# Up projection of a gated MLP with matmuls of 512 and 256 columns, and other short matmuls ahead of its units

## What is computed

```python
def conv_glu_ffn(h, w_up, w_conv, w_down):
    up = causal_dwconv(h @ w_up, w_conv)      # h (256, 2048), w_up (2048, 11264)
    g, u = jnp.split(up, 2, axis=-1)
    return (jax.nn.silu(g) * u) @ w_down      # w_down (5632, 2048)

x = x + conv_glu_ffn(rmsnorm(x, norm_ffn[l]), ffn_up[l], ffn_conv[l], ffn_down[l])
```

## Time and profile before

| | us |
|---|---|
| median of 3 runs | 1977.06 |
| lowest and highest run | 1976.96, 1981.57 |
| the profiled execution's own time | 1976.82 |
| its span in the trace | 1974.9 |
| PE busy | 1960.4 (99%) |
| DVE busy | 1179.8 (60%) |
| ACT busy | 868.4 (44%) |

### The profile page before, as it was taken

One profiled execution on the slowest core, in us unless ns is written; L12 is line 12 of the kernel. 1 busy time (PEld: TensorE's weight loads), 2 busy tenths in 40 slices (PEclk: granted clock), 3 DMA queues, 4 the chain that ended last, 5 costly groups with the idle time before them and its releaser, 6 DMA issues.

```text
span 1974.9 us, 38712 instructions
## 1 busy us (share of the span) xinstructions
PE 1960.4 (99%) x16939; PEld 1951.9 (99%) x16939; DVE 1179.8 (60%) x1292; ACT 868.4 (44%) x789; POOL 40.3 (2%) x62
## 2 busy tenths in 40 slices
PE   8999999999999999999999999999999999999999
PEld 8999999999999999999999999999999999999999
DVE  5677644545454376576655345777777777754443
ACT  5446334434374343455444444534344433333333
POOL 1000100000000000000000000000000000000000
PEclk9999999999999999999999999999999999999999
DMA  8666754665657757565564456665656565566664
GB/s 271 209 203 198 225 170 145 200 197 166 193 170 245 258 192 235 171 194 191 185 200 129 144 163 205 216 210 177 207 179 204 185 199 186 170 215 221 187 205 137
DMA packets 356648, 382.84 MB, mean 194 GB/s; under 512 B 8143, under 2 KB 351603, under 8 KB 355123
## 3 DMA queue, kind: packets, MB, share of 16 engines
q1 hardware_dynamic: 350947, 353.36, 56.2%
q0 software_dynamic: 5584, 27.70, 4.0%
HBM read 367.47 MB, written 13.58 MB: 193 GB/s over the span
## 4 chain that ended last, share of the span: by engine, by line
PE 96%; DVE 2%; DMA 1%; ACT 1%; issue 0%; SPq 0%; DVEq 0%; ACTq 0%
PE bank L1949 30%; PE bank L1950 30%; PE bank L1951 30%; DVE w_lo_home L1128 1%; PE bank L2373 1%; PE bank L2392 1%; DMA raw<-in_w_in 1%; PE bank L2146 1%; ACT w_hi_home L549 0%; PE bank L2192 0%; PE bank L2049 0%; PE bank L2140 0%; DMA ident<-in_shape_masks 0%; PE bank L2260 0%; PE bank L2054 0%
## 5 line engine op out<-in xcount | busy, mean ns | idle before, releaser
L1128 DVE TENSOR_TENSOR w_lo_home<-raw,w_hi_home 128x2048 fp32r<-128x2048 f32 (+1 forms) x349 | 756.9, 2169 | 619.3 <-ACT w_hi_home L549 619.0
L549 ACT ACTIVATE w_hi_home<-raw 128x2048 fp32r<-128x2048 f32 (+2 forms) x359 | 645.8, 1800 | 1043.3 <-PE bank L1951 1029.4
L1949 PE MATMUL bank<-x_home,w_hi_home 128*128 128x256 f32 x3712 | 1035.1, 279 | 3.1 <-DVE w_lo_home L1128 3.0
L1951 PE MATMUL bank<-x_home,w_lo_home 128*128 128x256 f32 x3712 | 1028.9, 277 | 0.0
L1950 PE MATMUL bank<-x_home,w_hi_home 128*128 128x256 f32 x3712 | 1028.9, 277 | 0.0
L1949 PEld LDWEIGHTS bank<-x_home,w_hi_home 128*128 128x128 f32 x3712 | 698.1, 188 | 4.7 <-issue 2.0
L1950 PEld LDWEIGHTS bank<-x_home,w_hi_home 128*128 128x128 f32 x3712 | 698.0, 188 | 0.2
L1951 PEld LDWEIGHTS bank<-x_home,w_lo_home 128*128 128x128 f32 x3712 | 698.0, 188 | 0.0
L1949 PE MATMUL bank<-act_hl,w_hi_home 128*128 128x256 f32 x704 | 196.5, 279 | 0.0
L1951 PE MATMUL bank<-act_hl,w_lo_home 128*128 128x256 f32 x704 | 195.1, 277 | 0.0
L1950 PE MATMUL bank<-act_hl,w_hi_home 128*128 128x256 f32 x704 | 195.1, 277 | 0.0
(11 more groups left out here) (317 smaller groups left out, 1745.1 us busy)
## 6 DMA issues: line engine op xcount, KB each, us to landing
raw<-in_w_in SPq DMA_DIRECT2D x52, 2048.0 KB, 8.7
raw<-in_ffn_up SPq DMA_DIRECT2D x44, 2048.0 KB, 8.0
raw<-in_ffn_down SPq DMA_DIRECT2D x32, 1408.0 KB, 6.5
raw<-in_xa_wkv SPq DMA_DIRECT2D x16, 2048.0 KB, 8.2
raw<-in_w_br SPq DMA_DIRECT2D x8, 2048.0 KB, 8.9
raw<-in_w_out SPq DMA_DIRECT2D x8, 2048.0 KB, 8.3
raw<-in_xa_wq SPq DMA_DIRECT2D x8, 2048.0 KB, 8.5
raw<-in_xa_wo SPq DMA_DIRECT2D x8, 2048.0 KB, 8.2
```

Source lines behind the costliest of these rows:

```text
L549: return nc.scalar.activation(out_, in_, func, **kw)
L1128: tt(split_out(w_lo, kind, half, at), halves(raw, kind, half, par), split_out(w_hi, kind, half, at).bitcast(f32), ALU.subtract).then_inc(l ...
L1949: mm(o, w[0], x[0], start=start, stop=False)
L1951: return mm(o, w[1], x[0], start=False, stop=stop)
```

## The change

UP no longer uses `three`. For each step k there are two matmuls: w_hi against both parts of the activations at once (512 moving columns, into the whole bank: hi x hi in columns 0 to 255, hi x lo in 256 to 511), and w_lo against the high part (256 columns, added to columns 256 to 511). So a bank ends with a major part left and a minor part right. ACT copies the minor part to a new tile (`minor_part`), DVE adds the two, and a further DVE instruction over 512 elements multiplies by `rstd`. The weights keep their place, 96 bytes on.

The short matmuls move: UP has two ahead of each of its units 3, 8, 13, 18, 23, 28 and 33, in thirteen forms; some that stood elsewhere are gone (A's second, BR's two, the wide ones of WO and XO, both at the start of DN), and BO's one stands ahead of its second half.

```diff
-UP_SETTLES = (3, 17, 31)
+UP_LEADS = (SETTLE, (LEAD_SMALL, (2, 64)), ((2, 2), (64, 64)), ((2, 128), (32, 32)), ((64, 2), (P, 64)), ((8, 8), (2, 32)), ((P, P), (16, 2)))
...
+            def minor_part(j, up):
+
+                par, h0 = slot_of("UP", up)
+                act.wait_ge(half_used, j * 4 + (4 * h0 + 2 * par + 2))
+                act.wait_ge(dve_evac, j * 2 + evacuated("UP", up)[1] - 1)
+                for x in range(2):
+                    last = copy(minor[:, x, :], up_bank(par, x)[:, SEQ:2 * SEQ])
+                last.then_inc(f_minor, 1)
...
+            minor_part(0, 0)
             act.wait_ge(spill, 32)
             with act.Fori(1, FC // 2) as j:
                 hi("UP", 2 * j, p0, j + h0)
+                minor_part(j - 1, 1)
                 silu_gate(j - 1)
                 hi("UP", 2 * j + 1, p1, j + h1)
+                minor_part(j, 0)
                 product_hi(j - 1)
             hi_half(*half_of(first_half("DN")))
             hi_half(*half_of(first_half("DN") + 1))
+            minor_part(FC // 2 - 1, 1)
             silu_gate(FC // 2 - 1)
...
                 dve.wait_ge(half_used, j * 4 + (4 * h0 + 2 * par + 2))
+                dve.wait_ge(f_minor, j * 2 + up + 1)
...
                 for x in range(2):
-                    last = tt(scaled[:, x * SEQ:(x + 1) * SEQ], up_bank(par, x)[:, 0:SEQ], rstd[:, :], ALU.mult)
+                    last = tt(scaled[:, x * SEQ:(x + 1) * SEQ], up_bank(par, x)[:, 0:SEQ], minor[:, x, :], ALU.add)
                 last.then_inc(dve_evac, 1)
+                dve.wait_ge(dve_evac, j * 2 + evacuated("UP", up)[1])
+                tt(scaled.rearrange("p (c s) -> p c s", c=2), scaled.rearrange("p (c s) -> p c s", c=2),
+                   bc(rstd[:, :].unsqueeze(1), [P, 2, SEQ]), ALU.mult).then_inc(f_scaled, 1)
...
-                    dve.wait_ge(dve_evac, j * 2 + evacuated("UP", up)[1])
+                    dve.wait_ge(f_scaled, j * 2 + up + 1)
...
+                    for k in range(KC if name == "UP" else 0):
+                        if parts and k == KC // 2:
+                            pe.wait_ge(lo_ready, whole)
+                        if ready and k % ready[2] == 0:
+                            pe.wait_ge(ready[0], ready[1] + k // ready[2] + 1)
+                        o = up_bank(par, half)
+                        at = place_of(name) + k * P
+                        mm(o[:, :].rearrange("p (j s) -> p j s", j=2), w_hi_home[:, half, at:at + P], acts[:, :, k, :],
+                           start=k == 0, stop=False)
+                        last = mm(o[:, SEQ:2 * SEQ], w_lo_home[:, half, at:at + P], acts[:, 0, k, :], start=False, stop=k == KC - 1)
...
-                product_half(m, lead={8: LEAD_WIDE, 9: LEAD_SMALL}.get(m))
+                product_half(m, lead=LEAD_WIDE if m == 8 else None)
...
-            project("BO", x_hl, 0, 1, leads=(LEAD_SMALL, None))
+            project("BO", x_hl, 0, 1, leads=(None, LEAD_SMALL))
...
-            project("BR", y_hl, 0, 1, leads=SETTLE)
-            project("BR", y_hl, 1)
+            project("BR", y_hl)
...
-            norm_beside(1, m + 2, x_hl)
+            norm_beside(1, m + 2, x_hl, (LEAD_SMALL, None, None))
...
-            product_half(m + 1, x_hl)
-
-            project("XO", x_hl, 1, 2, leads=SETTLE)
-            project("XO", x_hl, 2, COUNT["XO"] - 1)
+            product_half(m + 1, x_hl, lead=LEAD_SMALL)
+
+            project("XO", x_hl, 1, COUNT["XO"] - 1)
...
-            project("UP", x_hl, 1, UP_SETTLES[0])
-            for i, j in zip(UP_SETTLES, UP_SETTLES[1:] + (COUNT["UP"],)):
-                project("UP", x_hl, i, i + 1, leads=SETTLE)
-                project("UP", x_hl, i + 1, j)
+            project("UP", x_hl, 1, 3)
+            for n, leads in enumerate(UP_LEADS):
+                project("UP", x_hl, 3 + 5 * n, 4 + 5 * n, leads=leads)
+                project("UP", x_hl, 4 + 5 * n, 8 + 5 * n)
+            project("UP", x_hl, 3 + 5 * len(UP_LEADS))
...
-                settled = 0 if isinstance(c, int) and c == 0 else 2
+                settled = None if isinstance(c, int) and c == 0 else 2
```

More of the change, by code:

```diff
@@ L208, in build_program @@
         act_hl = sb("act_hl", [P, 2, FC, SEQ], f32r, d_scope)
+        minor = sb("minor", [P, 2, SEQ], f32, d_scope)
         d_scope.close()
@@ L315, in build_program @@
         f_c, f_g, f_s, f_p, f_h, f_l = (sem("ffn_" + n) for n in ("c", "g", "s", "p", "h", "l"))
+        f_minor, f_scaled = sem("ffn_minor"), sem("ffn_scaled")
         ot_t, ot_e = sem("ot_t"), sem("ot_e")
@@ L1985, in half_unit @@
                     cuts = (0, GH, GH + MH, KC) if kind == BR else (0, KC)
-                    out_of = lambda g: up_bank(par, half)[:, 0:SEQ] if name == "UP" else bank[par + 2 * g][:, half * SEQ:(half + 1) * SEQ]
                     if lead:
-                        lead_in(out_of(0), w_hi_home[:, half, place_of(name):], acts[:, 0, 0, :], lead)
-                    for k in ks:
+                        lead_in(up_bank(par, half)[:, 0:SEQ] if name == "UP" else bank[par][:, half * SEQ:(half + 1) * SEQ],
+                                w_hi_home[:, half, place_of(name):], acts[:, 0, 0, :], lead)
+                    for k in range(KC if name == "UP" else 0):
[8 more added lines that the diff above has]
+                        last = mm(o[:, SEQ:2 * SEQ], w_lo_home[:, half, at:at + P], acts[:, 0, k, :], start=False, stop=k == KC - 1)
+                    for k in ks if name != "UP" else ():
                         if parts and k == KC // 2:
@@ L1995, in half_unit @@
                         w = [t[:, half, k * P:(k + 1) * P] for t in (w_hi, w_lo)]
-                        last = three(out_of(g), w, [acts[:, j, k, :] for j in range(2)],
+                        last = three(bank[par + 2 * g][:, half * SEQ:(half + 1) * SEQ], w, [acts[:, j, k, :] for j in range(2)],
                                      k == cuts[g], k + 1 == cuts[g + 1])
@@ L2031, in transposes, with norm_beside @@
                     last.then_inc(tin_t, 1)
-            def norm_beside(k, m, acts):
-                leads = dict(zip((m + m % 2, m + m % 2 + 1), SETTLE))
+            def norm_beside(k, m, acts, leads):
                 for j in range(3):
-                    product_half(m + j, acts, lead=leads.get(m + j))
+                    product_half(m + j, acts, lead=leads[j])
                 product_half(m + 3, acts, ks=range(KC // 2))
@@ L2344, in _ @@
             product_half(m + 1, x_hl)
-            norm_beside(1, m + 2, x_hl)
+            norm_beside(1, m + 2, x_hl, (LEAD_SMALL, None, None))
             m = first_half("K")
             product_half(m, mem_hl, (n_lo, 0, 4))
-            norm_beside(2, m + 1, mem_hl)
+            norm_beside(2, m + 1, mem_hl, (None, LEAD_WIDE, LEAD_SMALL))
             product_half(m + 9, mem_hl)
@@ L2471, in down_pair @@
                             if k == 0 and g == settled:
-                                lead_in((o if g == 0 else bank[5])[:, 0:SEQ], w_hi_home[:, half, at:], x[:, 0, :], SETTLE[half])
+                                lead_in(bank[5][:, 0:SEQ], w_hi_home[:, half, at:], x[:, 0, :], SETTLE[half])
                             w = [t[:, half, at:at + P] for t in (w_hi_home, w_lo_home)]
```

## The result

The changed kernel takes 1995.88 us (median of 4 runs, 1991.82 to 1999.44), the kernel before in the same comparison 1978.47 (median of 4, 1976.96 to 1981.57): a ratio of 1.0088, interval 1.0074 to 1.0103. The forecast was 1968.1 with a range up to 1975.5, so the time lies outside it and the sign is the other one. It is rival 4 that came, with its 1995.

What follows compares the result with a forecast made beforehand. PE's instruction stream was taken as the bound: 1976.82 - 15.1 (pairs) - 1.5 (slow stretches) + 10.6 (DVE wait) - 3.0 (short matmuls) = 1967.8, plus 0.24 to compare with the median: 1968.1 us, range 1958.5 to 1975.5.

Steps and rivals of the forecast that it cites:

- rival 4: In UP, 512 columns cost more than two times 256: a pair of 356 ns, 1995 us in all; chance 0.05.
- The bound: Whole kernel: PE, busy 1960.4 of 1974.9 us, sets the end; the distance between the starts of two matmuls counts.
- The pair: UP's two matmuls per step: 216 + 113.3 = 329.3 ns instead of 340.0, over 1408 steps 15.1 us less.
- The pace: UP's 256-column matmuls counted at the fast 113.3 ns, not 117.8; its slow stretches gone, 1.5 us less.
- rival 1: UP's pairs run in the slow pace, 333.8 ns a pair, 1973.0 us in all; chance 0.25.
- DVE's wait: UP: PE waits for DVE's low part 0.53 us once in each of 20 rounds, 10.6 us more.
- The short matmuls: Moving or removing them changes nothing in UP and gives 3.0 us less in the other stages.
- A's second one: Stage A: its second short matmul goes with the slow stretch behind it, 1.2 us less.
- Six stand ahead of even ones: UP: six of fourteen short matmuls cost 0.11 us each, as many as before, so no change.
- BR and WO: Short matmuls and a slow half go in each stage: 0.4 us less in BR, 0.3 in WO.
- DN: Stage after UP: 0.4 us less without its short matmuls, if UP ends in the fast pace.

## Why the prediction was wrong

**The bound** was right: PE's instruction stream sets the end, and the distance between starts is what counts.

**The pair** is the step that failed: 329.3 ns in the sum, 353.3 on the chip, 24.0 x 1408 = 33.8 us. It failed in two places. First, 216 for the long matmul was taken from float32 rows. Those stream 256 columns in instructions that last twice as long, and there 217 ns hold; a matmul of fp32r with 512 columns never came under 224, in any kernel. Two different ways to stream were set equal because their lengths were near. The Trainium skill has the same figure on its page "TensorE: Matmul & The Clock Gate", section Back-to-back issue gap (215.8 ns for 512 columns); for fp32r no run here agrees with it. Second, "Behind the 256-column matmul of the pair the next load still has only that matmul's time" made the load the reason of the 113.3 ns. The kernels with weights of 4 columns refute it: the stream has 113.3 by itself. Then two fast short ones are 226.7, a long one is about that too, and 340.0 is left of a pair as of three, before any loss. From the earlier trace rows alone this could not be told, since every matmul there had its load; but the prediction could have held the two readings apart, and given the one under which joining gains nothing a chance of its own. It stood only as part of rival 4. Of the 24.0 ns, 10.7 are this saving that doesn't exist, and 13.3 are the pace.

**The pace** was to be the fast one, and rival 1 (0.25) gave its opposite. Pairs with full loads run slow in every kernel with the weights at 96 and the activations at 32, with either set of short matmuls, apart from a step or two behind each interruption. That is 1408 x 13.3 = 18.7 us, the whole of UP's loss. Rival 1 had only the short matmul of the pair slow, 333.8 ns; in the runs the long one is slow too. So rival 1's state and rival 4's size came together.

**Rival 4** had the right time with part of a wrong reason. Its pair of 356 ns was worked out as two slow matmuls and a third at 120; measured are 235.1 + 118.2. That its 1995 is so near is partly luck: the pair was 2.7 ns too dear, 3.8 us, and the other terms, -4.5 in its sum, come to +3.9 in the profiled execution (22.6 - 18.7). The point from which it decides, a pair of some 347 ns, agrees with the weights at 0, 346.8 ns and 1988.13 us against 1981.07, on one execution each. The two pieces of the activations, which it named, cost nothing.

**DVE's wait**, 10.6 us, did not come. Its own terms were near, as the timeline of DVE in the changed kernel shows for the end of a round, against the earlier trace rows:

```profile
1534.87 0.75 DVE L1858 TENSOR_TENSOR tmp<-bank,minor 128x256 f32<-128x256 f32 x2
1535.65 0.69 DVE L1861 TENSOR_TENSOR tmp<-tmp,rstd 128x512 f32<-128x512 f32 x1
1536.26 0.68 DVE L1893 TENSOR_TENSOR act_hl<-tmp,act_hl 128x512 f32 x1
...
1538.97 2.28 DVE L1143 TENSOR_TENSOR w_lo_home<-raw,w_hi_home 128x2048 fp32r<-128x2048 f32 x1
```

From the additions to product_lo it is 1.39 us instead of the forecast 1.50, and the low part ends at 1541.25. The weight load that needs it, and its matmul, start at 1541.64 and 1541.76:

```profile
1541.64 0.19 PEld L2015 LDWEIGHTS bank<-x_home,w_hi_home 128*128 128x128 f32 x1
```

The room is 0.39 us, where it was 0.69: 0.72 longer on DVE, and two halves of PE 2 x 16 x 13.3 ns = 0.43 longer. The sign of the halves' length was wrong because the pair's was. In the kernel with the long matmuls alone, where a half is short, the waits are there (64.0 us). By its trace PE loses some 2.6 us once in a round ahead of the first half of even units, where the prediction had its wait, and some 0.8 at each half of odd units, where it had none. So the chain exists, but it isn't the only one.

**The short matmuls.** A's second one went as forecast: the stretch behind the first stays fast, and the changed kernel's lead over the one before grows by 1.2 us there (from 0.5 at 69 us to 1.7 at 104). Other stretches change their pace both ways behind it: up to 610 us the lead lies between 0.3 and 1.7. "Six stand ahead of even ones... as many as are there now: nothing", and the same for the odd ones, was wrong for three matmuls (9.9 us in UP, in the kernel with the short matmuls alone) and without meaning for pairs. BR and WO, forecast at -0.7, came out slow for 1147 matmuls. DN, forecast at -0.4, starts in the slow pace as the prediction said it would if UP ends slow, and has 1.6 us more.

**What stays open.** Why there are two paces, and what decides which one comes after an interruption. The runs exclude the weight load as what sets the fast one, the two pieces as what makes pairs slow, the granted clock (1.00 in windows of both paces) and the DMA traffic (windows of either pace with 190 to 210 GB/s). They show that the distance between weights and activations and the load beside the stream both move the slow one, and that other placements have other paces (117.3, 118.7, 120.0). Loads between 4 and 64 columns are untested. The fast and the slow stretches of BR, of Q and K, and behind one and the same short matmul differ from kernel to kernel in ways that none of this explains.

## What to carry to other kernels

Here, joining two matmuls that share their weights could save only what the second load and the second instruction cost, and that was nothing. Measure it first, by shrinking the weights and looking whether the distance between the starts falls. If it doesn't, the number of columns is the price, and joining leaves it as it is. Take the time of a new shape from rows of the same number format, and give the case that it has no gain at all a chance of its own; and where a pace has two levels that any edit upstream can flip, count a gain only where the whole kernel keeps it, since the kernel with fewer short matmuls won some 3.4 us in the stretches it meant and lost most of it in others.

## What the runs showed of the hardware

- An fp32r matmul of 256 columns starts 113.3 ns after the one before at best, at a granted clock of 1.00 of 2.4 GHz, whether 128 or 4 weight columns load beside it; 512 columns take 224 to 241 ns, 235.1 in the mean of the changed kernel.
- At a granted clock of 0.50 (1.2 GHz) 512 columns take 427 ns, which is less than twice the 233 at 1.00.
- The recorded weight load takes 188 ns for 128 columns and 84 ns for 4. The fastest distance of the starts is the same with either.
- 768 fp32r columns in two instructions with 4-column loads never took less than 340 ns, the time of three fast matmuls of 256.
- With the pairs a step takes 353.3, 353.2, 350.5 and 346.8 ns with the weights at 96, 64, 32 and 0 bytes past 128 and the activations at 32, and 346.8 again at 96 and 0. The 340.0 of three fast matmuls, 346.8 and 353.3 lie some 6.7 ns apart; no run tells why.
- With loads of 64 columns a long stretch of 256-column matmuls ran at 119.0 ns, above the 117.8 of the slow stretches with loads of 128.
